# Layer 0's routing: the latents' lists sorted earlier, the last block of modulation products later, the first gather ahead of the late weight loads

## The chip, the cores and the metric

The kernel runs on one core of one Trainium2 chip. The metric is the device time of one execution in microseconds (us), lower is better. Every time below is that of one core.

## What is computed

A two-layer diffusion backbone over 512 latent tokens and 256 context tokens of width 1024. Each layer has a mixer (attention and a short convolution, ending in an output projection `w_out`) and an expert-choice mixture of experts (MoE). The part around the change is the seam between the two:

```python
x = x + g1 * ox                                   # ox: output projection
hx2 = _rmsnorm(x, norm2[l]) * (1.0 + sc2) + sh2
x = x + g2 * _ec_moe(hx2, router[l], ...)
...
def _ec_moe(h, router, w_gate, w_up, w_down):     # once for latents, once for context
    cap = CAPACITY_FACTOR * n // N_EXPERTS        # 64 of 512 latents, 32 of 256 context
    aff = softmax(h @ router)
    g, idx = top_k(swapaxes(aff, 1, 2), cap)      # per expert: its best tokens
    xs = h[idx]
    y = (silu(xs @ w_gate) * (xs @ w_up)) @ w_down * g
```

All scales and shifts (`sc2`, `sh2`, `g1` and so on) come from a modulation `silu(c) @ w_ada[l] + b_ada[l]`. Of the next layer's modulation the first 2048 columns are computed during this seam of layer 0.

## The kernel before

Every engine has its own instruction list, written out by hand; between them only semaphores set the order. The seam works on tiles of 128 tokens: layer 0 has six (t = 0 to 3 latents, t = 4 and 5 context), layer 1 has four (latents only). `NX` is 4, the number of latent tiles.

For each tile TensorE multiplies by `w_out` (`mixed_rows`, L1360, in pieces of k = 0 to 3, 4 to 5, 6 to 7). Behind the first piece of tile t stand the transposes of the normed tile t-1 (`turned_rows`, L1376), behind the second its router logits (`logit_parts`, L1388), behind the third their turn (`logits`, L1397). VectorE (DVE) scales and adds the residual (L1970, L1971, semaphore `x1`), takes a reciprocal (L1977) of the root that ScalarE (ACT) made of the squared sum (L1038, L1039), and writes half of the modulated transposed tile `o_h` (L1988); ACT writes the normed row (L1042, semaphore `oxn`) and the other half of `o_h` (L1050).

Between these DVE does two other works in layer 0:

- `ahead_sums(u)`, u = 0 to 7 (L1676): four products of 128x1024 with a summed output, next layer's modulation. Two units per latent tile, one after the reciprocal, one after `o_h`. Their weights come in 1 MB loads, two slots, issued by GpSimd (POOL) in `load_ahead` (L765).
- the latents' lists: `shifted`, `affinities` (softmax over experts, with ACT's Exp at L1045), the turn on TensorE (`turn_lists`, L1404), then eight rounds of `best_eight` (L1918 to L1921), each finding the next eight tokens of every half list. Rounds 0 to 3 stand in tile 4, rounds 4 to 7 in tile 5. Then `slots_out` (L1929, L1930), TensorE's `slots_across` (L1412, L1413), and `latents_merged` (L1942 to L1949), whose `iT` holds the token numbers.

POOL then copies the numbers of expert 0 (L817) and gathers its 64 latent rows of 4 KB from DRAM (L828); it has stored every tile's residual and normed rows (L793, L797) and waits for all of these stores first. TensorE turns the gathered rows (L1534), DVE modulates them (`first_latents`, L2075, L2076), and the MoE's first products start (`part_of`, L1510). The context's lists are sorted in four rounds around that.

SyncE (SP) loads all expert weights in units of 1 MB into a ring of 12 slots and some places of the arena that are free later. In layer 0 the units from the 13th on (`EARLY` is 0: four of `w_down`, two of `w_up`) wait until `o_h` and all the stores are done (L687 to L692), then they are issued.

Of the kernel before, what the change touches and what calls it, by code (L numbers as in the profile page):

```python
# [20 lines left out]
ALU = mybir.AluOpType  # L21
# [50 lines left out]
def build_program(nc, x, ctx, w_ada, w_adat, w_ahead, c_rows, w_in, w_out, router, w_gate, w_up, w_down, norm_final, small_in, rope, numbers, out):  # L72
# [102 lines left out]
    ahead_p = area(BIG + 16640, D).bitcast(BF16).rearrange("p (a k) -> p a k", a=2)  # L175
# [99 lines left out]
    s_ahead_c = sem("ahead_c_rows")  # L275
    s_ahead_mod = sem("ahead_mod_complete")
# [203 lines left out]
    LISTS_AT, MERGED_AT = 3840, 256  # L480
# [148 lines left out]
    def _(sp):  # L629
# [13 lines left out]
        for l in range(DEPTH):  # L643
# [33 lines left out]
            def load_long(which, expert, m0):  # L677
                for q in range(4):
                    m = m0 + q
                    dst, sem_of, _ = long_place(l, m)  # L680
                    if m < RING:
                        sp.wait_ge(free, spent(base) + m + 1 - RING)
                    elif m >= TURN[l]:
                        sp.wait_ge(free, spent(base) + m + 1 - TURN[l])
                    if m == RING + EARLY[l]:
                        sp.wait_ge(free, spent(where[("wout", l)]) + 4)
                        if l < DEPTH - 1:  # L687
                            sp.wait_ge(*LS[l]("ot", nq(l)))
# [21 lines left out]
    def _(pool):  # L710
# [28 lines left out]
        for l in range(DEPTH):  # L739
# [50 lines left out]
            for t in range(nq(l)):  # L790
                if l < DEPTH - 1:
                    pool.wait_ge(*L("x1", t + 1))
                    pool.dma_start(res[toks(t), :], o_x[t % 3]).then_inc(L[f"stx{t % 3}"], 16)  # L793
                    if 1 <= t < NX:
                        load_ahead(2 * t + 1)
                pool.wait_ge(*L("oxn", t + 1))
                pool.dma_start(xnd[toks(t), :], row_n(l, t)).then_inc(L[f"stn{t % 2}"], 16)  # L797
                if l < DEPTH - 1 and t < NX - 1:
                    load_ahead(2 * t + 2)
                if l < DEPTH - 1 and t + 3 < nq(l):  # L800
                    pool.wait_ge(*L(f"stx{t % 3}", 16 * (t // 3 + 1)))
                    pool.dma_start(o_x[t % 3], rows(t + 3)).then_inc(L[f"ox{t % 3}"], 16)
            for j in range(3 if l < DEPTH - 1 else 0):
                pool.wait_ge(*L(f"stx{j}", 16 * len(range(j, nq(l), 3))))
            for j in range(2):
                pool.wait_ge(*L(f"stn{j}", 16 * len(range(j, nq(l), 2))))
# [20 lines left out]
            if l < DEPTH - 1:  # L827
                pool.indirect_dma_start(out=xg[l][0:CAPX, :], out_offset=None, in_=xnd,  # L828
                                        in_offset=bass.IndirectOffsetOnAxis(ap=gidx[0:CAPX, 0:1], axis=0)
                                        ).then_inc(L["gl"], 16)  # L830
                pool.wait_ge(*L("ri", 2))
# [77 lines left out]
    def _(act):  # L909
# [11 lines left out]
        for l in range(DEPTH):  # L921
# [108 lines left out]

            act.wait_ge(s_norm[1], l + 1)
            for t in range(nq(l)):
                s = stream(t)
                act.wait_ge(*L("x1", t + 1))
# [8 lines left out]
                if t == NX:  # L1043
                    act.wait_ge(*L("asub", 1))
                    act.activation(aff[:, 0:NX, :], aff[:, 0:NX, :], ACT.Exp).then_inc(L["aexp"], 1)  # L1045
# [21 lines left out]
            n_col = 512 if l == DEPTH - 1 else 768  # L1067

# [19 lines left out]
    def _(pe):  # L1088
# [37 lines left out]
        for l in range(DEPTH):  # L1126
# [280 lines left out]
            def slots_across(g):  # L1407

                pe.wait_ge(*L("pad", g + 1))
                for r0 in list_groups(l)[g][2]:  # L1410
                    b, off = (5, 0) if r0 == 64 else (7 - r0 // 32, MERGED_AT)
# [4 lines left out]
            for i in range(nq(l) + 1):  # L1416
                if i < nq(l):
                    if i >= 2:
                        pe.wait_ge(*L("x1", i - 1))
                    mixed_rows(i, range(0, 4))  # L1420
# [4 lines left out]
                if i == NX + 1:  # L1425
                    turn_lists(0)
# [12 lines left out]
            else:  # L1439
                slots_across(0)  # L1440
# [158 lines left out]
    def _(dve):  # L1599
# [68 lines left out]
        def ahead_sums(u):  # L1668
# [3 lines left out]
            for o in range(4 * u, 4 * u + 4):  # L1672
# [3 lines left out]
                stt(ahead_p[:, o % 2, :], ahead_w[u % AHEAD_SLOTS][:, c % 2, :], 1.0, ahead_c[:, s, :], ALU.mult, ALU.mult,  # L1676
# [36 lines left out]
        for l in range(DEPTH):  # L1713
# [223 lines left out]
            low_v, low_i = [bank(7, NE, MERGED_AT + n * NE) for n in (0, 1)]  # L1937
            ctx_v, ctx_i = [bank(5, NE, n * NE) for n in (0, 1)]

            def latents_merged():  # L1940
                dve.wait_ge(*L("rows", 1))
                dlink(dve, dve.tensor_copy(high[:], bank(6, 2 * NE, MERGED_AT)))  # L1942
# [19 lines left out]
            for t in range(nq(l)):  # L1962
# [3 lines left out]
                if last and t >= 2:  # L1966
                    dve.wait_ge(*L("ot", t - 1))
                    dve.wait_ge(*L(f"stn{t % 2}", 16 * (t // 2)))
                part = row_n(l, t) if last else o_t
                dlink(dve, tt(part, bank(2 * (t % 2), D), g1row[s], ALU.mult))  # L1970
                tt(row_x(l, t), row_x(l, t), part, ALU.add).then_inc(L["x1"], 1)  # L1971
                if t == NX:
                    shifted(0)
                if t == NX + 1:
                    best_eight(0, 4)
                dve.wait_ge(*L("ort", t + 1))
                dve.reciprocal(stat[:, 2, t:t + 1], stat[:, 1, t:t + 1]).then_inc(L["orc"], 1)  # L1977
                if not last and t < NX:
                    ahead_sums(2 * t)
                if t == NX:  # L1980
                    affinities(0)
                if t == NX + 1:
                    best_eight(0, 5)
                dve.wait_ge(*L("ot", t + 1))
# [6 lines left out]
                if not last and t < NX:  # L1991
                    ahead_sums(2 * t + 1)
                if t == NX:
                    lists_in(0)
                    for r in range(4):
                        best_eight(0, r)
                if t == NX + 1:
                    best_eight(0, 6)
                    best_eight(0, 7)
# [7 lines left out]
            slots_out(0)  # L2007
# [80 lines left out]
            else:  # L2088
# [10 lines left out]
                first_context()  # L2099
            for e, par in body_experts(dve):  # L2100
# [96 lines left out]
```

## Time and profile before

| what | value |
|---|---|
| time before, median of 3 runs (lowest to highest) | 1933.68 us (1932.34 to 1934.58) |
| the profiled execution's own time | 1933.66 us |
| its span (first to last instruction) | 1931.5 us |
| TensorE busy | 1775.9 us, 92% of the span |
| DVE, ACT, POOL busy | 787.8, 369.1, 232.4 us |
| mean granted TensorE clock | 0.969 |
| layer 0's seam (first to last of its TensorE work) | about 399 to 527 us |
| layer 1's seam | about 1350 to 1445 us |

TensorE is busy for nearly the whole span, so what a change can win lies in the stretches in which it stands still. In a row of the timeline the bracket at the end tells how long the engine stood idle before it and what released it.

### The profile page before, as it was taken

To read this page: it belongs to the slowest core of one execution; us is meant where nothing else is said; L and a number is where in the kernel's file an instruction comes from. 1 tells how busy PE (TensorE), PEld (TensorE's weight loads), DVE (VectorE), ACT (ScalarE), POOL (GpSimd) and SP (SyncE) were. 2 spreads that over 40 slices of the span, in tenths; PEclk is the share of its full clock that TensorE was granted. 3 is DMA by queue.
4 is the path that set the end of the run, shared out by engine and by line. 5 is a ranking of instruction groups with operands and counts; after the bars stand their busy time and mean duration, and the time that the engine had idled before them with its cause. 6 is when DMAs were issued, how large, how long until landed. Compare 5 with 4: busy or idle time off the path is not lost.

```text
span 1931.5 us, 31131 instructions
## 1 busy us (share of the span) xinstructions
PE 1775.9 (92%) x13332; PEld 922.2 (48%) x13332; DVE 787.8 (41%) x1631; ACT 369.1 (19%) x801; POOL 232.4 (12%) x316
## 2 busy tenths in 40 slices
PE   6999999989599999999999999999949999889896
PEld 3886567744344444444443876577423332222221
DVE  2995665648611111111111664765242332323233
ACT  3213455622300000000001313555220000000001
POOL 1000330011011111212121001420000000000000
PEclk8999998999799999999999999999969999999998
DMA  9543000075779999999997843000579999999995
GB/s 386 217 153 153 1 1 1 2 319 204 267 276 393 396 393 396 392 395 393 393 393 312 317 167 131 1 23 25 218 286 388 404 404 413 404 410 404 411 412 232
DMA packets 83074, 525.69 MB, mean 272 GB/s; under 512 B 11280, under 2 KB 13600, under 8 KB 24064
## 3 DMA queue, kind: packets, MB, share of 16 engines
q1 hardware_dynamic: 65952, 476.17, 61.4%
q0 software_dynamic: 14784, 47.33, 7.9%
q8 instruction: 105, 1.72, 0.4%
q10 hardware_dynamic: 2208, 0.26, 0.1%
q14 instruction: 25, 0.20, 0.0%
HBM read 506.94 MB, written 16.79 MB: 271 GB/s over the span
## 4 chain that ended last, share of the span: by engine, by line
PE 75%; DMA 16%; DVE 4%; ACT 3%; issue 1%; SPq 0%; POOL 0%; DVEq 0%; ACTq 0%; POOLq 0%
PE psum L1471 16%; PE psum L1465 9%; PE psum L1474 8%; DMA ring<-in_w_up 7%; PE psum L1187 6%; PE psum L1360 6%; DMA arena<-in_w_up 6%; PE psum L1151 6%; PE psum L1263 5%; PE psum L1310 3%; PE psum L1281 3%; PE psum L1237 2%; PE psum L1553 2%; ACT arena L1004 2%; PE psum L1221 1%
## 5 line engine op out<-in xcount | busy, mean ns | idle before, releaser
L1471 PE MATMUL psum<-ring,arena 128*32 128x512 f32 x1920 | 250.4, 593 | 0.0
L1465 PE MATMUL psum<-ring,arena 128*64 128x512 f32 x976 | 228.5, 603 | 23.2 <-DMA ring<-in_w_down 12.9
L1072 ACT ACTIVATE arena<-psum 128x768 f32<-128x768 f32 (+1 forms) x32 | 22.5, 704 | 941.6 <-PE psum L1474 463.5
L1474 PE MATMUL psum<-ring,arena 128*32 128x256 f32 x1920 | 147.6, 379 | 0.0
L1465 PE MATMUL psum<-arena 128*64 128x512 f32 x560 | 132.2, 606 | 15.8 <-DMA arena<-in_w_down 6.6
L1360 PE MATMUL psum<-ring,arena 128*128 128x512 f32 x320 | 144.5, 603 | 0.0
L1465 PEld LDWEIGHTS psum<-ring,arena 128*64 128x64 f32 x976 | 63.8, 137 | 168.9 <-issue 117.7
L1004 ACT ACTIVATE arena<-psum,smx 128x768 f32<-128x768 f32 (+4 forms) x160 | 118.9, 748 | 107.6 <-DVE smx L1791 107.3
L1791 DVE TENSOR_REDUCE smx<-psum 128x1 f32<-128x768 f32 (+4 forms) x160 | 115.8, 765 | 39.0 <-PE psum L1221 27.9
L1474 PEld LDWEIGHTS psum<-ring,arena 128*32 128x32 f32 x1920 | 62.4, 110 | 143.6 <-issue 143.6
L1471 PE MATMUL psum<-arena 128*32 128x512 f32 x960 | 125.2, 593 | 0.0
L772 POOL TENSOR_SCALAR arena<-arena,smx 128x768 f32<-128x768 f32 (+1 forms) x40 | 77.9, 1947 | 368.9 <-DVE smx L1852 368.9
L1187 PE MATMUL psum<-ring,arena 128*128 128x256 f32 x544 | 120.8, 383 | 0.0
L1263 PE MATMUL psum<-arena,ring 128*128 128x512 f32 (+1 forms) x288 | 116.2, 545 | 1.6 <-ACT arena L1013 1.5
L1659 DVE SCALAR_TENSOR_TENSOR arena<-ring 128x1024 bf16<-128x1024 f32 x96 | 111.5, 1218 | 7.8 <-DMA ring<-in_w_adat 7.7
L1151 PE MATMUL psum<-ring,arena 128*128 128x256 f32 x512 | 114.0, 383 | 0.0
L2069 DVE TENSOR_TENSOR arena<-arena,psum 128x512 f32<-128x512 f32 x120 | 74.4, 681 | 89.1 <-PE psum L1553 89.1
L1187 PEld LDWEIGHTS psum<-ring,arena 128*128 128x128 f32 x544 | 103.8, 192 | 14.0
L1151 PEld LDWEIGHTS psum<-ring,arena 128*128 128x128 f32 x512 | 97.5, 192 | 13.0
L2060 DVE SCALAR_TENSOR_TENSOR arena<-psum,gcur,arena 128x512 f32<-128x512 f32 x15 | 11.3, 751 | 219.0 <-PE psum L1474 219.0
L1360 PEld LDWEIGHTS psum<-ring,arena 128*128 128x128 f32 x320 | 59.7, 193 | 68.0 <-issue 68.0
L2034 DVE TENSOR_TENSOR arena<-psum,arena 128x768 f32<-128x768 f32 (+1 forms) x32 | 26.4, 824 | 157.7 <-PE psum L1474 123.6
(286 smaller groups left out, 2067.3 us busy)
## 6 DMA issues: line engine op xcount, KB each, us to landing
ring<-in_w_gate SPq DMA_DIRECT2D x88, 1024.0 KB, 28.1
ring<-in_w_up SPq DMA_DIRECT2D x84, 1024.0 KB, 28.1
ring<-in_w_down SPq DMA_DIRECT2D x82, 1024.0 KB, 28.5
arena<-in_w_down SPq DMA_DIRECT2D x46, 1024.0 KB, 28.4
arena<-in_w_up SPq DMA_DIRECT2D x44, 1024.0 KB, 28.2
arena<-in_w_gate SPq DMA_DIRECT2D x40, 1024.0 KB, 28.5
ring<-in_w_adat SPq DMA_DIRECT2D x32, 1024.0 KB, 5.6
ring<-in_w_in SPq DMA_DIRECT2D x18, 1024.0 KB, 18.3
```

Source lines behind the costliest of these rows:

```text
L772: pool.tensor_scalar(p0, p0, smx[:, 2, u % 8:u % 8 + 1], None, ALU.mult).then_inc(L["first"], 1)
L1004: act.activation(p, scored(st, x), ACT.Exp, bias=smx[:, 0, u % 8:u % 8 + 1], accum_out=smx[:, 1, u % 8:u % 8 + 1]).then_inc(L["exp"], 1)
L1151: ins = mm(dst, hT[:, k, toks(t)], slot(where[("winA", l)] + j, 8)[:, k, :], start=k == 0, stop=k == KD - 1)
L1187: ins = mm(dst, hT[:, k, toks(t)], slot(where[("winD", l)] + j, 8)[:, k, :], start=k == 0, stop=k == KD - 1)
L1263: ins = mm(bank(6, n), slot(where[("winC", l, tile)], 8)[:, k, cc * P:(cc + 1) * P], hT[:, k, t0:t0 + n], start=k == 0, stop=k == KD - 1)
L1360: ins = mm(bank(2 * (t % 2) + n), mixc(k)[:, toks(t)], slot(wo + k // 2, 2)[:, k % 2, n * 512:(n + 1) * 512], start=k == 0, stop=k == KD - 1)
L1465: ins = mm(psum[64 * n:64 * n + 64, b * 512:(b + 1) * 512], lhs(k), w[:, n * 512:(n + 1) * 512], start=k == 0, stop=k == KD - 1)
L1471: ins = mm(psum[r0:r0 + 32, b * 512:(b + 1) * 512], lhs(k)[:, 32 * g:32 * g + 32], w[:, n * 512:(n + 1) * 512], start=k == 0, stop=k == KD ...
L1474: ins = mm(psum[32 * j:32 * j + 32, (b + 1) * 512:(b + 1) * 512 + 256], lhs_c(k), w[:, j * 256:(j + 1) * 256], start=k == 0, stop=k == KD - 1)
L1659: stt(products[:, o % 3, :], long_slot(l, u % LONG_SLOTS)[:, j, :], 1.0, c_row(l, s), ALU.mult, ALU.mult, accum_out=mod[:, l, LONG_CHUNK + ...
L1791: dve.tensor_reduce(smx[:, 0, u % 8:u % 8 + 1], scored(st, x), axis=AX_X if st.kind == "W" else AX_XY, op=ALU.max, negate=True).then_inc(L ...
L2069: ins = tt(half, half, bank(sums_at(part, blk, h)), ALU.add)
```

## The change

1. DVE, layer 0: of `ahead_sums` tile 0 has one unit instead of two, behind `o_h`. Every later unit stands one place later, and the last unit (7) stands behind the MoE's `first_context`. `load_ahead` moves accordingly on POOL, and the last unit's scratch `ahead_p` gets another place. ACT's first Silu waits for all sums.
2. DVE, tiles 4 and 5: `shifted` stands ahead of tile 4's residual, `affinities` ahead of its reciprocal, round 0 ahead of its `o_h`, rounds 1 to 4 behind it; rounds 5, 6, 7 and `slots_out` stand ahead of tile 5's `o_h`. TensorE turns the lists inside tile 5's first piece and does `slots_across` ahead of tile 5's logits. The merged lists lie in PSUM banks 3 and 2 instead of 7 and 6.
3. ACT: Sqrt's table is loaded once at the start of the seam; Exp for the latents stands ahead of tile 4, with Sqrt's table loaded again behind it; Exp's table is loaded right after the last tile's normed row.
4. POOL waits, before the first gather, for the stores of the four latent tiles only; it signals `s_first_gather` behind the gather, and SP's late loads wait for that too.

```diff
 # SP
                         sp.wait_ge(free, spent(where[("wout", l)]) + 4)
                         if l < DEPTH - 1:
+                            sp.wait_ge(s_first_gather, 1)
                             sp.wait_ge(*LS[l]("ot", nq(l)))
...
 # POOL
                     if 1 <= t < NX:
-                        load_ahead(2 * t + 1)
+                        load_ahead(2 * t)
                 pool.wait_ge(*L("oxn", t + 1))
                 pool.dma_start(xnd[toks(t), :], row_n(l, t)).then_inc(L[f"stn{t % 2}"], 16)
-                if l < DEPTH - 1 and t < NX - 1:
-                    load_ahead(2 * t + 2)
+                if l < DEPTH - 1 and 1 <= t < NX:
+                    load_ahead(2 * t + 1)
...
             for j in range(2):
-                pool.wait_ge(*L(f"stn{j}", 16 * len(range(j, nq(l), 2))))
+                pool.wait_ge(*L(f"stn{j}", 16 * len(range(j, NX, 2))))
...
                                         ).then_inc(L["gl"], 16)
+                pool.sem_inc(s_first_gather, 1)
+                for j in range(2):
+                    pool.wait_ge(*L(f"stn{j}", 16 * len(range(j, nq(l), 2))))
...
 # ACT
+            act.activation(rootx[:], eps[:], ACT.Sqrt)
             act.wait_ge(s_norm[1], l + 1)
             for t in range(nq(l)):
                 s = stream(t)
+                if t == NX:
+                    act.wait_ge(*L("asub", 1))
+                    act.activation(aff[:, 0:NX, :], aff[:, 0:NX, :], ACT.Exp).then_inc(L["aexp"], 1)
+                    act.activation(rootx[:], eps[:], ACT.Sqrt)
                 act.wait_ge(*L("x1", t + 1))
...
-                if t == NX:
-                    act.wait_ge(*L("asub", 1))
-                    act.activation(aff[:, 0:NX, :], aff[:, 0:NX, :], ACT.Exp).then_inc(L["aexp"], 1)
+                if t == nq(l) - 1:
+                    act.activation(rootx[:], eps[:], ACT.Exp)
...
+            if l < DEPTH - 1:
+                act.wait_ge(ahead_sum, 4 * AHEAD_UNITS)
...
 # TensorE
-                    mixed_rows(i, range(0, 4))
+                    if i == NX + 1:
+                        mixed_rows(i, range(0, 3))
+                        turn_lists(0)
+                        mixed_rows(i, range(3, 4))
+                    else:
+                        mixed_rows(i, range(0, 4))
...
-                if i == NX + 1:
-                    turn_lists(0)
+                if i == NX + 2:
+                    slots_across(0)
...
 # DVE
+                if t == NX:
+                    shifted(0)
                 part = row_n(l, t) if last else o_t
                 dlink(dve, tt(part, bank(2 * (t % 2), D), g1row[s], ALU.mult))
                 tt(row_x(l, t), row_x(l, t), part, ALU.add).then_inc(L["x1"], 1)
                 if t == NX:
-                    shifted(0)
-                if t == NX + 1:
-                    best_eight(0, 4)
-                dve.wait_ge(*L("ort", t + 1))
-                dve.reciprocal(stat[:, 2, t:t + 1], stat[:, 1, t:t + 1]).then_inc(L["orc"], 1)
-                if not last and t < NX:
-                    ahead_sums(2 * t)
-                if t == NX:
                     affinities(0)
                 if t == NX + 1:
                     best_eight(0, 5)
+                dve.wait_ge(*L("ort", t + 1))
+                dve.reciprocal(stat[:, 2, t:t + 1], stat[:, 1, t:t + 1]).then_inc(L["orc"], 1)
+                if not last and 1 <= t < NX:
+                    ahead_sums(2 * t - 1)
+                if t == NX:
+                    lists_in(0)
+                    best_eight(0, 0)
+                if t == NX + 1:
+                    best_eight(0, 6)
+                    best_eight(0, 7)
+                    slots_out(0)
                 dve.wait_ge(*L("ot", t + 1))
...
                 if not last and t < NX:
-                    ahead_sums(2 * t + 1)
+                    ahead_sums(2 * t)
                 if t == NX:
-                    lists_in(0)
-                    for r in range(4):
+                    for r in range(1, 5):
                         best_eight(0, r)
-                if t == NX + 1:
-                    best_eight(0, 6)
-                    best_eight(0, 7)
...
                 first_context()
+                ahead_sums(AHEAD_UNITS - 1)
```

DVE's list in layer 0, tile 0 and the start of tile 1, before. L1970 and L1971 are the residual, L1977 the reciprocal, L1676 the `ahead_sums` products, L1988 `o_h`:

```order
L1970 TENSOR_TENSOR arena<-psum,arena 128x1024 [waits ox0,po,gxe]
L1971 TENSOR_TENSOR arena<-arena 128x1024 [waits dve_chain]
L1977 RECIPROCAL stat<-stat 128x1 [waits ort]
L1676 SCALAR_TENSOR_TENSOR arena,mod<-arena 128x1024 [waits ahead_landed0,ahead_c_rows]
L1676 SCALAR_TENSOR_TENSOR arena,mod<-arena 128x1024
L1676 SCALAR_TENSOR_TENSOR arena,mod<-arena 128x1024 [waits ahead_sum] x2
L1988 TENSOR_SCALAR arena<-psum,acol,mod 128x128 [waits ot]
L1988 TENSOR_SCALAR arena<-psum,acol,mod 128x128 x3
L1676 SCALAR_TENSOR_TENSOR arena,mod<-arena 128x1024 [waits ahead_sum,ahead_landed1]
L1676 SCALAR_TENSOR_TENSOR arena,mod<-arena 128x1024 [waits ahead_sum] x3
L1970 TENSOR_TENSOR arena<-psum,arena 128x1024 [waits ox1,po]
```

And the same stretch in the changed kernel, where L1988, L1989, L1995, L2009 and L1692 are these lines:

```order
L1988 TENSOR_TENSOR arena<-psum,arena 128x1024 [waits ox0,po,gxe]
L1989 TENSOR_TENSOR arena<-arena 128x1024 [waits dve_chain]
L1995 RECIPROCAL stat<-stat 128x1 [waits ort]
L2009 TENSOR_SCALAR arena<-psum,acol,mod 128x128 [waits ot]
L2009 TENSOR_SCALAR arena<-psum,acol,mod 128x128 x3
L1692 SCALAR_TENSOR_TENSOR arena,mod<-arena 128x1024 [waits ahead_landed0,ahead_c_rows]
L1692 SCALAR_TENSOR_TENSOR arena,mod<-arena 128x1024
L1692 SCALAR_TENSOR_TENSOR arena,mod<-arena 128x1024 [waits ahead_sum] x2
L1988 TENSOR_TENSOR arena<-psum,arena 128x1024 [waits ox1,po]
```

Tile 0's `o_h` no longer stands behind a product that waits for a load, and the tile has four products instead of eight.

DVE's list at the end of the seam, from tile 5's residual add on, before (L1918, L1919, L1921 are one round, L1929 and L1930 `slots_out`):

```order
L1971 TENSOR_TENSOR arena<-arena 128x1024 [waits dve_chain]
L1918 MAX vals<-arena 48x8
L1919 MAX_INDEX idx<-vals,arena 48x8 [waits dve_chain]
L1921 MATCH_REPLACE arena<-vals,arena 48x256 [waits dve_chain]
L1977 RECIPROCAL stat<-stat 128x1 [waits ort,dve_chain]
L1918 MAX vals<-arena 48x8
...
L1988 TENSOR_SCALAR arena<-psum,acol,mod 128x128 [waits lg,ot,dve_chain]
L1988 TENSOR_SCALAR arena<-psum,acol,mod 128x128 x3
L1918 MAX vals<-arena 48x8
...
L1918 MAX vals<-arena 48x8 [waits dve_chain]
L1919 MAX_INDEX idx<-vals,arena 48x8 [waits dve_chain]
L1929 COPY vpad<-vals 16x128 [waits dve_chain]
```

And in the changed kernel (L1989 the residual add, L1934 to L1937 one round, L1945 and L1946 `slots_out`, L2009 `o_h`):

```order
L1989 TENSOR_TENSOR arena<-arena 128x1024 [waits dve_chain]
L1934 MAX vals<-arena 48x8
...
L1995 RECIPROCAL stat<-stat 128x1 [waits ort,dve_chain]
L1934 MAX vals<-arena 48x8
...
L1934 MAX vals<-arena 48x8 [waits dve_chain]
L1935 MAX_INDEX idx<-vals,arena 48x8 [waits dve_chain]
L1945 COPY vpad<-vals 16x128 [waits dve_chain]
L1946 TENSOR_SCALAR vpad<-vals 16x128
L1945 CAST ipad<-idx 16x128
L1946 TENSOR_SCALAR ipad<-idx 16x128
L2009 TENSOR_SCALAR arena<-psum,acol,mod 128x128 [waits lg,ot]
```

Behind the residual add there were four rounds, two of them behind `o_h`; now there are three, and `slots_out` stands ahead of `o_h`.

## Rows read from the trace of the kernel before

**Rows 1.** TensorE's waits, 395 to 560 us: total, times, longest.

```profile
PE psum L1534 <- DMA arena<-normed_rows,gidx: 7.6, 1, 7.6
PE psum L1388 <- DVE arena L1988: 6.3, 2, 4.8
```

**Rows 2.** Timeline, tiles 0 to 4: start, us, what, idle before.

```profile
397.70 1.07 POOL L765 DMA_DIRECT2D arena<-in_w_ahead  x2
...
420.98 3.60 PE L1360 MATMUL psum<-ring,arena 128*128 128x512 f32 x8
...
423.28 1.23 DVE L1676 SCALAR_TENSOR_TENSOR arena<-arena 128x1024 bf16<-128x1024 f32 x1 [4.47 <-DMA arena<-in_w_ahead]
...
427.86 1.37 DVE L1988 TENSOR_SCALAR arena<-psum,acol,mod 128x128 f32<-128x128 f32 x4
...
429.38 1.08 PE L1388 MATMUL psum<-arena,rout 128*32 128x128 f32 x16 [4.80 <-DVE arena L1988]
...
436.06 7.11 PE L1360 MATMUL psum<-ring,arena 128*128 128x512 f32 x16
...
439.43 0.53 POOL L765 DMA_DIRECT2D arena<-in_w_ahead  x1
...
443.88 3.60 PE L1360 MATMUL psum<-ring,arena 128*128 128x512 f32 x8
...
446.41 1.23 DVE L1676 SCALAR_TENSOR_TENSOR arena<-arena 128x1024 bf16<-128x1024 f32 x1 [0.23 <-DMA arena<-in_w_ahead]
...
451.67 7.11 PE L1360 MATMUL psum<-ring,arena 128*128 128x512 f32 x16
...
482.87 7.11 PE L1360 MATMUL psum<-ring,arena 128*128 128x512 f32 x16
```

**Rows 3.** Windows: us, busy by engine, granted clock, DMA share, GB/s.

```profile
425.00:430.00 5.00, 0.62 (x13) 0.66 (x16) 5.00 (x11) 0.00 (x0) 0.53 (x1) 0.76 1.00 397
```

**Rows 4.** DMA issues, 395 to 440 us: count, KB each, median us to landing.

```profile
arena<-in_w_ahead POOLq DMA_DIRECT2D x4, 1024.0 KB, 16.6
```

**Rows 5.** Timeline, tile 5 and the routing behind it.

```profile
498.86 1.23 DVE L1970 TENSOR_TENSOR arena<-psum,arena 128x1024 f32<-128x1024 f32 x1 [0.31 <-DVE arena L1921]
...
502.55 1.28 ACT L1039 ACT_TABLE_LOAD   x1
...
505.64 1.55 PE L1376 MATMUL psum<-ident,arena 128*128 128x128 f32 x8 [4.64 <-ACT arena L1042]
...
508.57 0.41 DVE L1918 MAX8 vals<-arena 48x8 f32<-48x256 f32 x1
...
511.02 0.21 DVE L1929 COPY vpad<-vals 16x128 f32<-16x128 f32 x1
...
513.09 0.19 DVE L1942 COPY high<-psum 128x32 f32<-128x32 f32 x1 [1.16 <-PE psum L1413]
...
514.01 0.17 DVE L1947 CAST iT<-token 64x16 uint32<-64x16 f32 x1
...
514.38 0.17 DVE L1885 TENSOR_REDUCE affm<-psum 128x2 f32<-128x32 f32 x1
...
515.11 0.97 POOL L828 DMA_INDIRECT arena<-normed_rows,gidx  x1 [0.58 <-POOL gidx L817]
...
519.42 0.40 DVE L1921 MATCH_REPLACE8 arena<-vals,arena 16x256 f32<-16x256 f32 x1
...
524.00 1.09 PE L1534 MATMUL psum<-ident,arena 64*128 64x64 f32 x8 [7.61 <-DMA arena<-normed_rows,gidx]
...
526.71 6.97 PE L1510 MATMUL psum<-ring,arena 128*32 128x512 f32 x48 [1.62 <-issue]
```

**Rows 6.** Timeline of SP in layer 0's seam.

```profile
509.12 2.00 SPq L693 DMA_DIRECT2D arena<-in_w_down  x4
```

**Rows 7.** Timeline, layer 1: its first gather of 64 rows.

```profile
1438.92 0.98 POOL L823 DMA_INDIRECT arena<-normed_rows,gidx  x1 [0.28 <-POOL gidx L817]
...
1442.83 1.11 PE L1450 MATMUL psum<-ident,arena 64*128 64x64 f32 x8 [3.78 <-DMA arena<-normed_rows,gidx]
```

**Rows 8.** Timeline, start of layer 0's MoE.

```profile
548.07 1.02 DVE L2020 TENSOR_TENSOR arena<-psum,acol 128x512 f32<-128x512 f32 x2 [5.25 <-PE psum L1450]
...
551.44 1.04 PE L1471 MATMUL psum<-ring,arena 128*32 128x512 f32 x8
```

More of the change, by code:

```diff
@@ L174, in build_program @@
     ahead_c = area(BIG + 14336, 2, D)
-    ahead_p = area(BIG + 16640, D).bitcast(BF16).rearrange("p (a k) -> p a k", a=2)
+    ahead_p = [area(at, D).bitcast(BF16).rearrange("p (a k) -> p a k", a=2) for at in (BIG + 16640, BIG + 7424)]
     sqd = area(BIG + 8448, 2, T)
@@ L275, in build_program @@
     s_ahead_c = sem("ahead_c_rows")
+    s_first_gather = sem("first_gather_issued")
     s_ahead_mod = sem("ahead_mod_complete")
@@ L478, in list_groups @@
         return [latents, (NX, NB, (64,), CAPC)] if l < DEPTH - 1 else [latents]
-    LISTS_AT, MERGED_AT = 3840, 256
+    LISTS_AT = 3840
     def signals(l):
@@ L827, in _ @@
             if l < DEPTH - 1:
-                pool.indirect_dma_start(out=xg[l][0:CAPX, :], out_offset=None, in_=xnd,
+                pool.indirect_dma_start(out=xg[l][0:CAPX, :], out_offset=None, in_=xnd[0:SEQ, :],
                                         in_offset=bass.IndirectOffsetOnAxis(ap=gidx[0:CAPX, 0:1], axis=0)
                                         ).then_inc(L["gl"], 16)
+                pool.sem_inc(s_first_gather, 1)
+                for j in range(2):
+                    pool.wait_ge(*L(f"stn{j}", 16 * len(range(j, nq(l), 2))))
                 pool.wait_ge(*L("ri", 2))
@@ L1410, in slots_across @@
                 for r0 in list_groups(l)[g][2]:
-                    b, off = (5, 0) if r0 == 64 else (7 - r0 // 32, MERGED_AT)
+                    b, off = (5, 0) if r0 == 64 else (3 - r0 // 32, 0)
                     mm(bank(b, NE, off), vpad[r0:r0 + NE, :], sel[r0:r0 + NE, :], start=True, stop=True)
@@ L1439, in _ @@
             else:
-                slots_across(0)
                 turn_lists(1)
@@ L1675, in ahead_sums @@
                     dve.wait_ge(ahead_sum, o - 1)
-                stt(ahead_p[:, o % 2, :], ahead_w[u % AHEAD_SLOTS][:, c % 2, :], 1.0, ahead_c[:, s, :], ALU.mult, ALU.mult,
+                stt(ahead_p[u == AHEAD_UNITS - 1][:, o % 2, :], ahead_w[u % AHEAD_SLOTS][:, c % 2, :], 1.0, ahead_c[:, s, :], ALU.mult, ALU.mult,
                     accum_out=mod[:, 1, c, s:s + 1]).then_inc(ahead_sum, 1)
@@ L1935, in slots_out @@
                 ins.then_inc(L["pad"], 1)
-            low_v, low_i = [bank(7, NE, MERGED_AT + n * NE) for n in (0, 1)]
+            low_v, low_i = [bank(3, NE, n * NE) for n in (0, 1)]
             ctx_v, ctx_i = [bank(5, NE, n * NE) for n in (0, 1)]
@@ L1941, in latents_merged @@
                 dve.wait_ge(*L("rows", 1))
-                dlink(dve, dve.tensor_copy(high[:], bank(6, 2 * NE, MERGED_AT)))
+                dlink(dve, dve.tensor_copy(high[:], bank(2, 2 * NE)))
                 tt(first[:], low_v, high[:, 0:NE], ALU.is_ge)
@@ L2006, in _ @@
                     best_eight(0, r)
-            slots_out(0)
+                slots_out(0)
             latents_merged()
```

## The prediction

> **What bounds the kernel now.** TensorE is busy for 92% of the span, so I asked where it stands still. Its list of waits over layer 0's seam names two places that matter: 7.6 us for the first gather, and 6.3 us for DVE's `o_h`, 4.8 of them at once [rows 1]. I then followed each in the timeline.
>
> The first place is tile 0. TensorE ends the second piece of tile 1 at 420.98 + 3.60 = 424.58 and stands until 429.38, because DVE writes tile 0's `o_h` only at 427.86: ahead of it stand four `ahead_sums` products, which began at 423.28, when their weights landed [rows 2]. There the granted clock is 0.76 on average, so it is at the lower of its two levels (1.2 GHz) for part of that stretch [rows 3], and the rest of tile 1 is slow.
>
> The second place is the end of the seam. From tile 5's residual at 498.86 a single chain runs: residual, ACT's root with a table load of 1.28, normed row, transposes at 505.64, `o_h`, two rounds of the sort, `slots_out` at 511.02, merge, `iT` at 514.01, gather issued at 515.11. The gathered rows are used only at 524.00, and the MoE starts at 526.71 [rows 5]. SP issued its late loads of 1 MB from 509.12 on, ahead of the gather [rows 6]. Layer 1's gather of the same 64 rows took 1442.83 - 1438.92 = 3.91 from its issue to TensorE's first use, against 524.00 - 515.11 = 8.89 in layer 0 [rows 7, 5].
>
> What lies behind the seam frees ring slots only as TensorE goes on, and SP loads only into freed slots, so I take it that all of it moves as a whole when the MoE starts earlier.
>
> **Part 1: tile 0's order.** Without a stall it takes 451.67 - 443.88 = 7.79 from the start of a second piece to the next tile. In tile 1 it took 436.06 - 420.98 = 15.08 [rows 2]. With `o_h` right behind the transposes DVE would write it from about 421.1 on, for 1.37, before TensorE asks at 424.58. The gain is 15.08 - 7.79 = **7.3 us**: the wait of 4.8, and 2.5 of work at the lower clock.
>
> What is late next? The four products of unit 0 last 427.86 - 423.28, about 4.6 [rows 2], to 427.9. Tile 2 would start at 420.98 + 7.79 = 428.8, so 0.9 of cover is left. In tiles 1 to 3 DVE still has two units each, and every load takes another's old place in both lists: the unit used behind `o_h` is now issued right behind the residual's store, where the one issued at 439.43 was used at 446.41 after a wait of 0.23 [rows 2]. The first of them may come 1 us late, since POOL is held by tile 0's store until the burst of loads has drained; I put DVE's spare time at 0.5 and TensorE's at 1.2 per tile and cost it at nothing, bounded by 1.
>
> Unit 7 moves behind `first_context`: 4.6, and about 0.4 for bias and scales, 5.0 in all. DVE is idle there for 5.25 before expert 1's rows, and TensorE wants these at 551.44, 1.3 after DVE has them (548.07 and two steps of 1.02) [rows 8]. Cost nothing, bounded by 0 and 1. ACT's first Silu waits for these sums too; it is wanted at 551.44 as well.
>
> **Part 2: tile 4**, in the old time base. TensorE starts tile 5's first piece at 482.87 and ends it 7.11 later, at 490.0 [rows 2]. DVE puts `shifted` (0.5) ahead of the residual. From a residual's start to the transposes it takes 505.64 - 498.86 - 1.28 = 5.50 without a table load [rows 5], so the normed row is there at 482.9 + 0.5 + 5.5 = 488.9, 1.1 before it is wanted. The softmax (0.8 behind the residual's 2.5) ends at 486.7; the turn wants it three quarters into the piece, at 488.2. ACT's two switches (1.28 each) and Exp end at 485.6, as the residual does at 485.9. DVE then has the lists at 489.0, round 0 until 490.5, `o_h` until 492.5 and four rounds of about 1.5, until 498.4; the residual waits for TensorE until 498.86 as before. Nothing is lost, with margins of 0.3 to 1.5.
>
> **Part 3: from 498.86 on.** The table load is gone, so the transposes start at 505.64 - 1.28 = 504.4. DVE has rounds 6 and 7 from 503.1 on (511.02 - 508.57 = 2.45 for a long and a short one), `slots_out` from 505.6, and the merge could start 513.09 - 511.02 = 2.07 later, at 507.7; `o_h` lies in between and ends at 507.9. The merge takes 514.18 - 513.09 = 1.09: `iT` at 509.0 instead of 514.2. With the same 0.93 for POOL's copy the gather is issued at **509.9** instead of 515.11 [rows 5], 5.2 earlier. Tile 5's residual store is still waited for; I take it to have landed by then, since SP waited for it too and issued at 509.12 [rows 6].
>
> Then the gather itself. The late loads are held until it is issued, so I take layer 1's 3.91: rows at 513.8 instead of 524.00. Now DVE is later than they are: the context's list starts with the last logits at about 510.1 and takes 519.82 - 514.38 = 5.44 to the end of its second round [rows 5], to 515.5, and `first_latents` stands behind it. From the transposes' end to the first product it was 526.71 - 525.09 = 1.6, so the MoE starts at 517.1 instead of 526.71: **9.6 us**.
>
> The late loads are issued 1.8 later than before, at 510.9. Six of them, 6.3 MB at the 397 GB/s of [rows 3], take 16, to 527. `w_down` of expert 0 is used behind 551.44 in the old order [rows 8], behind 541.8 in the new. The cover is some 15 us.
>
> **Part 4: tables in layer 1.** Exp's load there lay almost beside DVE's work and tile 0's Sqrt load beside matmuls. I give 0.2, bounds 0 and 1.3 (one load).
>
> A rule weighed. In the row the load takes 1.28, and the 5.50 above takes off no more [rows 5]. The Trainium skill ("ScalarE: Activation LUTs", What ACT_TABLE_LOAD costs) adds a drain of about 1380 ns to the load's 1283, 2.66 us per switch. By that, taking one away in tile 5 would give 1.4 more, and the two in tile 4 would take 5.3 and end behind the residual, which would eat the margin there; the trace of before has no such gap around its load.
>
> **The sum.** 7.3 + 9.6 + 0.2 = 17.1, against the profiled execution's own 1933.66 (the runs' median is 1933.68, so nothing to correct): 1916.6.
>
> **The rivals.**
>
> *The gather isn't protected.* SP issues as soon as the gather's instruction is through. If its loads crowd the rows as now, the gather keeps its 8.89: 509.9 + 8.9 = 518.8, and 2.7 to the first product, 521.5. The gain there is 5.2, in all 12.7: **1921.0**. For it: the loads and the gather share the DMA engines. Against it: the loads start behind the rows, not ahead. Chance 0.17.
>
> The Trainium skill ("DMA: Bandwidth & Descriptors", Queues, rings and completion order) says that a DMA engine goes round robin between its queues, packet by packet. By this a burst ahead or behind would cost 64 rows little, and holding back the loads would win little by itself, as in this rival; the 8.89 against 3.91 speaks against it.
>
> *Tile 0's stall only moves*, to tile 1's `o_h`. Only 9.8 is left: **1923.9**. Against it: 0.9 us to spare above. Chance 0.07; both this and the one before, 1928.3, chance 0.02.
>
> *The gap is short enough to keep the clock.* TensorE stands for 3.4 instead of 4.64 before the transposes; work at the upper level would give 1 to 2.5 more, about **1915**. Chance 0.10.
>
> *Slower: late modulation loads.* In the burst the first load, issued at 397.70, was used at 423.28 [rows 2], and the median to landing was 16.6 [rows 4], against 7.0 in the quiet case. If the loads behind the residual's store took 16.6 in tiles 1 to 3, each tile would lose 9.6 less 1.2: 25 in all, 1916.6 + 25 = **1942**. It decides from 17.1 / 3 + 1.2 + 7.0 = 14 us per load on. Against it: the burst has drained by tile 1's end, and later tiles load the same amount as before. Chance 0.03 for slower, 0.02 for a partial case within 0.2%.
>
> **The numbers.** The forecast has 0.59, the rivals what is given. A measurement of this kernel can tell about 0.2%, 3.9 us, from no change. Faster 0.95, same 0.02, slower 0.03. The range reaches from the kept clock to the unprotected gather, with 1 us beyond each: 1914 to 1922. Outside lie the 1923.9 case, the double one and the slow ones.
>
> **What the profile after would show.** No wait of TensorE for `o_h` in tile 0, and its clock whole between 425 and 435; tile starts 15.6 apart and 7.3 earlier from tile 2 on; no table load between tile 5's residual and its normed row; the gather issued 5.2 + 7.3 = 12.5 before 515.11, at 502.6, its rows used 4 us later or when DVE is through the context's second round; the first product at about 509.8; SP's late loads right behind the gather; no new wait for expert 1's rows. I am wrong if the gather still takes 8 us, if a modulation load makes `o_h` late in tiles 1 to 3, or if TensorE waits for `afft` in tile 5.

## The result

The changed kernel takes 1925.83 us (median of 8 runs, 1922.01 to 1930.63) beside 1936.68 for the kernel before on the same chip (8 runs): ratio 0.9946, 95% interval 0.9933 to 0.9959. It is faster by 0.54%, about 10.5 us (the medians lie 10.85 apart), where 17.1 were forecast, and lies outside the range. Its profiled execution took 1923.94 us, span 1922.1.

The difference lies in layer 0's seam. I measure it from the gate transposes (TensorE turns the mixer's gate `g1` into rows, the seam's first step; 395.61 us before, 396.79 after) to the MoE's first product (526.71 and 517.41): 131.10 before, 120.62 after, 10.5 less. Behind it the two spans run 1404.8 and 1404.7; ahead of it the changed kernel was 1.2 us later in its profiled execution, in work that the change doesn't touch. The gate transposes, before and after:

```profile
395.61 3.84 PE L1333 MATMUL psum<-ident,mod 128*128 128x128 f32 x32 [0.38 <-DVE arena L1807]
...
396.79 3.84 PE L1345 MATMUL psum<-ident,mod 128*128 128x128 f32 x32 [0.38 <-DVE arena L1823]
```

TensorE's waits in the stretch of [rows 1], of the kernel after:

```profile
PE psum L1550 <- DMA arena<-normed_rows,gidx: 6.4, 1, 6.4
PE psum L1388 <- ACT arena L1052: 5.6, 2, 3.4
PE psum L1526 <- issue: 1.6, 1, 1.6
PE psum L1416 <- DVE afft L1910: 1.5, 1, 1.5
PE psum L1400 <- DVE arena L2009: 0.5, 2, 0.4
```

The 6.3 for `o_h` are down to 0.5, as meant. The gather's wait is still 6.4, where 7.6 stood before, and `L1388 <- ACT` comes twice, where one (3.4) was expected. Two things went otherwise than forecast, then.

The window of [rows 3], after. TensorE is busy throughout, at the upper level:

```profile
425.00:430.00 5.00, 5.00 (x29) 2.42 (x28) 4.01 (x9) 0.28 (x1) 0.00 (x0) 1.00 1.02 404
```

The timeline of tiles 0 to 3 after, POOL, DVE and TensorE (compare [rows 2]):

```profile
420.19 0.53 POOL L799 DMA_DIRECT2D normed_rows<-arena  x1 [2.40 <-ACT arena L1052]
433.38 0.53 POOL L804 DMA_DIRECT2D arena<-in_x  x1 [12.66 <-DMA residual<-arena]
433.90 0.53 POOL L795 DMA_DIRECT2D residual<-arena  x1
434.42 0.53 POOL L767 DMA_DIRECT2D arena<-in_w_ahead  x1
...
422.15 1.37 DVE L2009 TENSOR_SCALAR arena<-psum,acol,mod 128x128 f32<-128x128 f32 x4 [3.44 <-PE psum L1388]
424.12 1.23 DVE L1692 SCALAR_TENSOR_TENSOR arena<-arena 128x1024 bf16<-128x1024 f32 x1 [0.61 <-DMA arena<-in_w_ahead]
...
444.63 1.23 DVE L1692 SCALAR_TENSOR_TENSOR arena<-arena 128x1024 bf16<-128x1024 f32 x1 [4.78 <-DMA arena<-in_w_ahead]
...
429.72 7.11 PE L1372 MATMUL psum<-ring,arena 128*128 128x512 f32 x16
...
445.33 7.11 PE L1372 MATMUL psum<-ring,arena 128*128 128x512 f32 x16
454.64 1.09 PE L1388 MATMUL psum<-ident,arena 128*128 128x128 f32 x8 [2.20 <-ACT arena L1052]
455.57 3.60 PE L1372 MATMUL psum<-ring,arena 128*128 128x512 f32 x8
...
463.58 7.11 PE L1372 MATMUL psum<-ring,arena 128*128 128x512 f32 x16
```

`o_h` is written at 422.15, ahead of the products, and tile 2 starts at 429.72 instead of 436.06. But the products of unit 2 wait 4.78 at 444.63 for a load that POOL issued at 434.42. POOL stood from 420.72 to 433.38 for the landing of tile 0's residual store, and the load now has its place behind that wait and behind tile 1's residual store. Tile 2's normed row comes late by this, TensorE waits 2.20 for it at 454.64, and tile 4 starts at 463.58, 18.25 behind tile 3 instead of 15.60.

The end of the seam after (compare [rows 5] and [rows 6]):

```profile
499.42 1.15 ACT L1052 ACTIVATE arena<-arena,stat 128x1024 f32<-128x1024 f32 x1 [0.30 <-DVE stat L1995]
500.58 1.28 ACT L1054 ACT_TABLE_LOAD   x1
501.88 0.20 ACT L1054 ACTIVATE rootx<-eps 128x1 f32<-128x1 f32 x1
...
500.62 1.97 PE L1388 MATMUL psum<-ident,arena 128*128 128x128 f32 x8 [3.35 <-ACT arena L1052]
...
504.89 0.17 DVE L1963 CAST iT<-token 64x16 uint32<-64x16 f32 x1
...
505.84 1.97 SPq L695 DMA_DIRECT2D arena<-in_w_down  x4
...
505.99 0.97 POOL L830 DMA_INDIRECT arena<-normed_rows,gidx  x1 [0.58 <-POOL gidx L819]
...
514.70 1.08 PE L1550 MATMUL psum<-ident,arena 64*128 64x64 f32 x8 [6.38 <-DMA arena<-normed_rows,gidx]
515.89 0.69 DVE L2092 TENSOR_TENSOR arena<-psum,acol 128x512 f32<-128x512 f32 x1 [4.14 <-PE psum L1550]
...
517.41 7.07 PE L1526 MATMUL psum<-ring,arena 128*32 128x512 f32 x48 [1.62 <-issue]
```

The gather is issued 109.20 behind the gate transposes; before it was 119.50. But SP's first late load begins at 505.84, 0.15 ahead of the gather's own row, and the gather takes 514.70 - 505.99 = 8.71, where 8.89 stood before.

The steps between follow. The second gates are TensorE's next such transposes, behind tile 5 (498.83 before, 495.09 after).

| step, us | before | after | gain | forecast |
|---|---|---|---|---|
| gate transposes to tile 2 | 40.45 | 32.93 | 7.52 | 7.3 |
| tile 2 | 15.61 | 15.61 | 0 | 0 |
| tile 3 | 15.60 | 18.25 | -2.65 | 0, at most -1 |
| tile 4 to the second gates | 31.56 | 31.51 | 0.05 | 0 |
| second gates to tile 5's transposes | 6.81 | 5.53 | 1.28 | 1.3 |
| from there to the gather's issue | 9.47 | 5.37 | 4.10 | 3.9 |
| issue to first use | 8.89 | 8.71 | 0.18 | 5.0 |
| first use to the first product | 2.71 | 2.71 | 0 | -0.6 |

### The profile page after: what moved, and what is told of

It reads as the page before. It is cut to its first block, busy times and chain, and to the rows that moved or that the text cites. A ratio compares the mean times of both kernels' runs of the same rounds, so it can differ in the third digit from the quotient of the medians.

```text
span 1922.1 us, 31140 instructions
## 1 busy us (share of the span) xinstructions
PE 1776.2 (92%) x13332; PEld 923.5 (48%) x13332; DVE 788.4 (41%) x1631; ACT 370.2 (19%) x806; POOL 232.5 (12%) x316
## 4 chain that ended last, share of the span: by engine, by line
PE 74%; DMA 17%; DVE 5%; ACT 3%; issue 1%; SPq 0%; POOL 0%; DVEq 0%; POOLq 0%; ACTq 0%
PE psum L1487 16%; PE psum L1481 9%; PE psum L1490 8%; DMA ring<-in_w_up 7%; PE psum L1199 6%; DMA arena<-in_w_up 6%; PE psum L1163 6%; PE psum L1372 5%; PE psum L1275 5%; PE psum L1322 3%; PE psum L1293 3%; PE psum L1249 2%; PE psum L1569 2%; ACT arena L1009 2%; PE psum L1233 1%
## 5 line engine op out<-in xcount | busy, mean ns | idle before, releaser
L1163 PEld LDWEIGHTS psum<-ring,arena 128*128 128x128 f32 x512 | 98.5, 194 | 13.2
```

The costliest lines, as they stand in the source:

```text
L1163: ins = mm(dst, hT[:, k, toks(t)], slot(where[("winA", l)] + j, 8)[:, k, :], start=k == 0, stop=k == KD - 1)
```

## The experiments

Theory A: the late loads get ahead of the gather, since the signal that frees them comes too early. Its rival B: layer 0's gather is slow by itself. Theory C: POOL, held by the residual store, issues unit 2's load too late. Its rival D: the DMA engines can't bring that load earlier. The ratios are to the kernel before, run on the same chip; seams and their parts come from one profiled execution of each kernel.

### The hold moved to the landing, and taken away

```diff
--- e1_loads_after_rows, against the changed kernel
-                            sp.wait_ge(s_first_gather, 1)
+                            sp.wait_ge(*LS[l]("gl", 16))
...
-                pool.sem_inc(s_first_gather, 1)
```

> The changed kernel, but SP's late loads wait until the first gather's rows have landed, not only for the signal behind its issue. Theory A (the 8.7 us of the gather come from the late loads, which start before its rows are through): the gather takes about 3.9 us from issue to first use as in layer 1, DVE's second context round (ends 5.4 us behind the last logits) then holds first_latents, and the MoE starts some 4.2 us earlier than in the changed kernel: about 1921.6 against its 1925.8 in the timed runs; no later wait appears, since expert 0's w_down has some 10 us of cover left. Theory B (layer 0's gather is slow by itself, for example because its rows were only just stored): it keeps 8 to 9 us, and the time stays within 1 us of the changed kernel's.

Measured: 1923.59, ratio 0.9943 (0.9929 to 0.9956). TensorE in tile 3, then the gather with POOL, SP and TensorE:

```profile
454.33 1.92 PE L1387 MATMUL psum<-ident,arena 128*128 128x128 f32 x8 [2.28 <-ACT arena L1051]
456.04 4.50 PE L1371 MATMUL psum<-ring,arena 128*128 128x512 f32 x8
...
507.13 0.97 POOL L830 DMA_INDIRECT arena<-normed_rows,gidx  x1 [0.58 <-POOL gidx L819]
...
511.41 1.92 SPq L695 DMA_DIRECT2D arena<-in_w_down  x4
...
511.48 1.09 PE L1549 MATMUL psum<-ident,arena 64*128 64x64 f32 x8 [2.02 <-DMA arena<-normed_rows,gidx]
```

The gather takes 4.35 instead of 8.71: A, not B. From its issue to the first product it is now 7.32, 4.1 less. Tile 3, though, took 19.78 here, 1.5 more than in the changed kernel, so the seam is only 2.6 shorter (118.05), and the ratio shows no difference; about 4.2 us were expected. The 1.5 come from TensorE's clock: it waits 2.28 here and 2.20 in the changed kernel, but the granted clock in 450 to 460 us is 0.83 here and 1.00 there, and the same work that takes 1.09 and 3.60 us there takes 1.92 and 4.50 here.

e2_no_hold takes away both the wait and the signal.

> The changed kernel without SP's wait for the gather's signal: the late loads go as soon as tile 5's stores have landed, some 2 us before the gather's issue. Theory A: they are further ahead of the gather's rows; 8.7 to 9.5 us from issue to use. If the signal did protect the gather by some amount, that amount is lost here. Theory B: the gather's 8.7 unchanged. In both the seam's end moves by less than 1 us, since the signal came at 505.84, before the gather's own span began at 505.99, and so held the loads back by only some 2 us.

One run, 1928.88. The loads begin 2.16 ahead of the gather, which takes 9.21. The hold as it was written moved the loads by 2.0 us and is worth 0.5 us at most: the four kernels with it took 8.55 to 9.03 (the table at the end), which is as wide a scatter. The seam is 124.56, because tile 3 took 21.69 here.

### The signal behind an operation that POOL's pipe must finish

```diff
--- e3_signal_behind_alu, against the changed kernel
-                pool.sem_inc(s_first_gather, 1)
+                pool.tensor_tensor(perch[:, 3, :], perch[:, 4, :], perch[:, 4, :], ALU.add).then_inc(s_first_gather, 1)
```

> The changed kernel, but the signal hangs on a small GpSimd operation behind the gather, which starts when the gather's span of about 1 us is over. Theory A in the form that the signal only came too early: SP's loads start some 1.2 us later, behind all of the gather's descriptors, and the gather needs 3.9 to 5 us. Theory A in the form that the loads crowd the rows even from behind: the gather still takes 6 to 8.7 us. Theory B: 8.7 unchanged.

One run, 1924.84. POOL, SP and TensorE at the gather:

```profile
508.58 0.99 POOL L830 DMA_INDIRECT arena<-normed_rows,gidx  x1 [0.58 <-POOL gidx L819]
509.58 0.18 POOL L833 TENSOR_TENSOR perch<-perch 1x2 f32<-1x2 f32 x1
...
509.84 2.27 SPq L695 DMA_DIRECT2D arena<-in_w_down  x4
...
513.05 1.09 PE L1550 MATMUL psum<-ident,arena 64*128 64x64 f32 x8 [2.13 <-DMA arena<-normed_rows,gidx]
```

The added operation runs only when the gather's row has ended, and SP starts 1.26 behind the start of that row instead of 0.15 ahead of it. That is enough: the gather takes 4.47, and 7.33 to the first product, the same as with the hold to the landing. The seam stays at 120.62, since unit 2's load made DVE wait 6.83 here and TensorE 4.24, with work at the lower clock behind it; tile 3 took 22.36, and the second fault took back what mending the first gave.

### The kernel before with the landing's hold alone

```diff
--- e7_before_held, against the kernel before
                         if l < DEPTH - 1:
+                            sp.wait_ge(*LS[l]("gl", 16))
```

> The kernel before, in its old order, with one line more: SP's late loads wait until the first gather's rows have landed. Theory A: the gather takes 3.9 to 4.4 us instead of 8.9, the context's two rounds are over by then (5.4 us from their start at the merge), so the seam from gate transposes to the first product shrinks from 131.1 by 4.5 to 5.2 us, to about 126.3, with nothing of the change in it; some 1931 in the timed runs where the kernel before has 1935.4. Theory B (the faster gather needs something else of the changed kernel): 131.

Measured: ratio 0.9982 (0.9969 to 0.9996). The gather takes 3.89, as in layer 1 [rows 7], and the seam 125.40, which is 5.7 less (1.0 of it ahead of tile 2). From the gather's issue to the first product it is 6.59 instead of 11.60: one line is worth 5.0, about half of what the whole change gave in the seam.

### Unit 2's load in time

```diff
--- e4_unit2_early, against the changed kernel
-                    if 1 <= t < NX:
+                    if 2 <= t < NX:
                         load_ahead(2 * t)
...
-                if l < DEPTH - 1 and 1 <= t < NX:
-                    load_ahead(2 * t + 1)
+                if l < DEPTH - 1 and t < NX:
+                    load_ahead(2 * t + 1 if t else 2)
```

> The changed kernel, but POOL issues the load of modulation unit 2 already in tile 0 (behind its normed row's store, when unit 0 is summed, ahead of the residual load for tile 3). Theory C (the 4.8 us that DVE waits for it come from POOL standing 12.7 us for the first residual store, so that the load goes out at 434.4 together with four others): the load goes out at about 429, DVE's wait and TensorE's 2.2 us in tile 2 vanish, tile 3 starts 2.6 us earlier, about 1923.2 in the timed runs. Theory D (the DMA engines cannot bring unit 2 any earlier, since the burst is still draining): DVE still waits 2 us or more and TensorE's start of tile 3 gains under 1 us.

Measured: 1921.72, ratio 0.9931 (0.9917 to 0.9945). POOL's timeline, and the starts of tiles 3 and 4 on TensorE:

```profile
428.18 0.54 POOL L767 DMA_DIRECT2D arena<-in_w_ahead  x1 [8.62 <-DVE arena L1692]
432.81 0.53 POOL L804 DMA_DIRECT2D arena<-in_x  x1 [4.09 <-DMA residual<-arena]
...
444.17 7.11 PE L1372 MATMUL psum<-ring,arena 128*128 128x512 f32 x16
459.77 7.11 PE L1372 MATMUL psum<-ring,arena 128*128 128x512 f32 x16
```

Issued at 428.18, as soon as unit 0 has freed the slot and ahead of the wait for the store, the load is there when DVE wants it; neither DVE nor TensorE waits, and the tiles stand 15.6 apart. The seam is 118.30. Not D; and C, in that the load must stand ahead of that wait. The gather, unprotected here, takes 9.03.

### Part 1 alone, as it is and mended

e5_products_only is the kernel before with the changed places of the loads and products. e10_products_unit2_early adds the edit of e4.

> The kernel before with the first part of the change alone: the modulation products and their loads one place later, unit 7 behind first_context. By the trace of the changed kernel: TensorE's wait in tile 0 and its slow clock are gone (7.5 us from the gate transposes to tile 2's start), and DVE's wait for unit 2's load takes 2.2 to 4.2 us of it back in tile 2. From the gate transposes to the MoE's first product 131.1 us in the kernel before; here 125.3 to 126.8. If the late load came from the rest of the change (its other store and table order) and not from this part, the full 7.5 stands: 123.6. The rest of the seam as before: a table load in tile 5's chain, the gather 8.9 us.

> The kernel before with part 1 alone (as e5_products_only) and unit 2's load issued in tile 0 behind the normed store. Theory C (GpSimd, held for the first residual store, issues unit 2's load too late, and this is what took part 1's 7.3 back): the 5.68 us wait of VectorE for that load goes, tile 3 to 4 takes 15.6 instead of 20.6, the seam is 124.0 instead of 129.05, and the ratio is 0.9964 (0.995 to 0.998). Theory D (the DMA engines could not bring it earlier, whenever it is issued): VectorE still waits 3 us or more there, the seam stays above 127, the ratio 0.998 to 1.000.

Measured: 0.9990 (0.9977 to 1.0003) without the edit, 0.9962 (0.9945 to 0.9979) with it. Without it, POOL's and DVE's timeline:

```profile
435.06 0.54 POOL L802 DMA_DIRECT2D arena<-in_x  x1 [12.04 <-DMA residual<-arena]
...
436.11 0.53 POOL L765 DMA_DIRECT2D arena<-in_w_ahead  x1
...
446.74 1.23 DVE L1679 SCALAR_TENSOR_TENSOR arena<-arena 128x1024 bf16<-128x1024 f32 x1 [5.68 <-DMA arena<-in_w_ahead]
```

Tile 2 begins 7.3 earlier in both. Without the edit tile 3 takes 20.60, and 5.0 are given back, more than in the changed kernel; the seam is 129.05, above the 125.3 to 126.8 expected. With it tile 3 takes 15.61 and the seam is 123.67, 7.4 less than before's. So the order of tile 0 is worth its 7.3 only when the load behind it is moved too.

### Parts 2 and 3 without part 1

e8_lists_only and e8b_lists_only put the ahead units' loads and products back into their old places. The two have the same instructions. In the first, unit 7's scratch lies over rows of the gate (`g1row`) that are still in use; the second has the old scratch.

> The changed kernel with the modulation products and their loads in the old places (two units from tile 0 on, none behind first_context): the lists, tables and the signal alone. TensorE stands 4.8 us in tile 0 again, with the slow clock. From there on the trace of the changed kernel applies: 1.3 us for the table load out of tile 5's chain, 4.1 for slots_out ahead of o_h and the merge ahead of the logits, nothing at the gather. 131.1 - 5.5 = 125.6 from the gate transposes to the first product. If unit 7's products in tile 3 delayed the lists in tile 4, more would be lost: 127 or over.

> The change without part 1: the products and loads of the ahead units in their old places (unit 7 in tile 3 with the scratch it had before), everything else as in the changed kernel. This is e8_lists_only with unit 7's scratch moved so that nothing is overlaid. If the parts add up: tile 2 starts 39.8 to 40.5 us behind the gate transposes, the gather takes 8.7 to 9.2, the seam is 125.1, that is 6.0 less than before's 131.1, and the ratio is about 0.9970 (0.9955 to 0.9985). If the parts interact (the old tile 0 stall loosens or tightens later loads): the seam is off 125.1 by more than 1.5.

Measured: one run of 1931.11 for the first; ratio 0.9968 (0.9956 to 0.9980) for the second, seams 125.07 and 125.33. The gather is issued at 114.07 instead of 119.50 and takes 8.55. The parts add up nearly: 5.8 us here and 7.4 in e10 make 13.2, and e4, which has both, gained 12.8 (0.32% and 0.38% against 0.69%).

### Both faults mended

e9_both_mended is the changed kernel with the edits of e3 and e4.

> The changed kernel with both faults mended: the signal behind a small GpSimd operation, so that the late loads come 1.3 us later, and unit 2's load issued in tile 0. Both gains add: 118.3 (unit 2 early alone) less 4.1 = 114.2 us from the gate transposes to the first product, against 131.1 before: 16.9 us, the size of the forecast. In the timed runs 1935.4 - 16.9 = 1918.5, a ratio of 0.9913. If the two are not independent (the drained DMA queue of the one being needed by the other), it stays at 116 or more.

Measured: 1918.28, ratio 0.9913 (0.9899 to 0.9928), the fastest of all. POOL, SP, TensorE and DVE at the gather:

```profile
503.99 0.99 POOL L830 DMA_INDIRECT arena<-normed_rows,gidx  x1 [0.58 <-POOL gidx L819]
504.99 0.18 POOL L833 TENSOR_TENSOR perch<-perch 1x2 f32<-1x2 f32 x1
...
505.25 2.49 SPq L695 DMA_DIRECT2D arena<-in_w_down  x4
...
508.42 1.09 PE L1550 MATMUL psum<-ident,arena 64*128 64x64 f32 x8 [2.10 <-DMA arena<-normed_rows,gidx]
511.32 5.35 PE L1526 MATMUL psum<-ring,arena 128*32 128x512 f32 x24 [1.81 <-issue]
...
509.36 0.40 DVE L1937 MATCH_REPLACE8 arena<-vals,arena 16x256 f32<-16x256 f32 x1
509.80 0.69 DVE L2092 TENSOR_TENSOR arena<-psum,acol 128x512 f32<-128x512 f32 x1
```

The seam takes 113.88, 17.2 less than before; the medians lie 16.2 apart. `first_latents` now stands behind the second round of the context's list without a wait of its own, as the prediction had it, and the first product comes 7.33 behind the gather's issue (7.2 forecast).

## Why the prediction was wrong

**What bounds the kernel** and **all of it moves as a whole** held: the gain is the seam's. Behind the seam the profiled executions scatter from 1404.7 to 1410.6 without a pattern, so less than that isn't to be read there in one execution.

**Part 1, 7.3 us**: measured 7.52, and 7.3 in e5 and e10. The clock is whole in 425 to 430, and unit 0's products end at 428.8, 0.9 ahead of tile 2's start, the cover that was counted on.

**"The first of them may come 1 us late ... I ... cost it at nothing, bounded by 1"**: this is the first step that failed, in size. The mechanism was named, POOL held by tile 0's store, but its price wasn't worked out from the rows. DVE wanted the load at 444.63 - 4.78 = 439.85, and it was issued at 434.42. With the 7.0 of the quiet stretch it would have been there at 441.4, 1.6 late, not far from the 1 I had. But it took 10.2, 3.2 more, and the two make the wait of 4.8. I had taken the duration from a quiet stretch, though the wait in front of it ends in a burst. TensorE loses 2.65 in the changed kernel, 4.2 in e1, 5.0 in e5, 6.1 in e2 and 6.8 in e3, whose order is the same there. In these four it waits 2.28, 3.09, 2.93 and 4.24, and the rest is mostly work at the lower clock (granted 0.83 in e1 and 0.66 in e3 over 450 to 460 us, 1.00 in the changed kernel, which waits 2.20); the bound of 1 had no term for that. What stretches the load is, most likely, that POOL lets everything go at once. The DMA view of 428 to 450 us of the changed kernel (22 us in 40 slices, then the issues):

```profile
GB/s 395 410 335 402 328 410 350 201 22 30 15 0 209 141 276 276 365 432 365 305 313 223 253 290 320 350 402 410 439 432 387 402 417 246 164 112 60 45 22 0
...
arena<-in_w_ahead POOLq DMA_DIRECT2D x2, 1024.0 KB, 9.8
arena<-in_x POOLq DMA_DIRECT2D x1, 512.0 KB, 4.8
residual<-arena POOLq DMA_DIRECT2D x1, 512.0 KB, 5.5
normed_rows<-arena POOLq DMA_DIRECT2D x1, 512.0 KB, 10.4
arena<-in_ctx POOLq DMA_DIRECT2D x1, 512.0 KB, 9.9
```

The engines all but stand still for some 2 us (slices 9 to 12) until POOL is free; then six transfers, 4 MB in all, are issued within 6.4 us. With the load ahead of all that, in e4, e9 and e10, the loss is gone. That the company is what stretches a load is argued, not tested by itself: in e4, where unit 2's load isn't among the six, unit 3's, issued at 437.70 in the middle of the others, lands 7.9 behind its issue, where the two loads of the changed kernel need 10.2 and 9.5. Why the same load takes 9.7 (e1) to 11.5 us (e3) between kernels alike in this stretch isn't settled.

**The slower rival** ("late modulation loads", from 14 us per load on) is this mechanism in three tiles. The load took about 10, under the 14 it needed, and only tile 3 was hit: later loads are issued without a held POOL. The rival that the stall moves to tile 1's `o_h` was wrong in place: the load late next was the one two units on. That its 1923.9 is the profiled execution's 1923.94 is chance.

**Part 2, nothing lost**: 31.51 against 31.56 us. Tile 4's residual waits 0.44 for the fifth round, which costs TensorE nothing.

**Part 3 up to the gather's issue, 5.2**: 5.4 (1.28 and 4.10). TensorE stands 3.35 instead of 4.64 [rows 5] and then works at the lower clock (0.61 in 500 to 502, 0.50 from 502 to 514), so the case that the clock is kept didn't come. The 1.28 of the load are all that went: the activation behind the load at 500.58 starts at 501.88, with 0.02 between. The row ahead of the load ends at 500.57, so there is no gap on that side either. The drain of about 1380 ns that the Trainium skill adds to the load ("ScalarE: Activation LUTs", What ACT_TABLE_LOAD costs) doesn't show in this trace.

**"The late loads are held until it is issued, so I take layer 1's 3.91"**: this is the step that failed and cost most. The first rival, with 0.17, had it that the gather isn't protected. Its reason against, "the loads start behind the rows, not ahead", is what the trace refutes: the signal passes the gather. Mended, the gather takes 4.4 (3.9 where the loads wait for the landing), so the 3.91 itself was a fair price.

Together: 1916.6 + 4.8 (gather 8.71 instead of 3.91) + 2.65 (tile 3) = 1924.05, and the profiled execution took 1923.94. That it fits to 0.1 is partly luck: parts 1 and 3 gave 0.4 more than forecast, the step to the first product cost 0.6 less, and against these stand 1.2 lost ahead of the seam. With both faults mended the seam's forecast is met, and part by part: 7.5 up to tile 2, 5.4 up to the gather's issue and 4.3 from there to the first product, against 7.3, 5.2 and 4.4.

**Unit 7 behind `first_context`, nothing**: right. Its products run 533.54 to 538.2, expert 1's rows follow at 538.90, and TensorE has no wait there. **Part 4, 0.2**: nothing that small can be read behind the seam.

## What to carry to other kernels

A signal that stands in program order behind a DMA's issue is no proof that the DMA is ahead in the engines; put it on an operation that waits for the issue to be through, or wait for the landing, and look in the trace at which row comes first. When work is taken from an in-order queue and put behind another wait, follow that wait to its end in the trace and price the load from there, with all that is let go at the same moment; a bound of "at most 1" needs rows of its own. And measure a change's parts alone: here one part gave back 5.0 of its own 7.3, and two small edits took the gain from 0.54% to 0.87%.

## What the runs showed of the hardware

The gather of 64 rows costs one of two prices, by when SP's burst of 1 MB loads begins relative to the start of its own row (us, from issue to TensorE's first use):

| kernel | burst begins | gather |
|---|---|---|
| e5, e10 | -6.69 | 8.76, 8.34 |
| before | -5.99 | 8.89 |
| e2 | -2.16 | 9.21 |
| after, e4, e8, e8b | -0.15 | 8.71, 9.03, 8.93, 8.55 |
| e3, e9 | +1.26 | 4.47, 4.43 |
| e7, e1 | +3.81, +4.28 | 3.89, 4.35 |

Between -0.15 and +1.26 it falls by half, and neither an earlier nor a later start matters much. A burst that begins while the gather is still under way, at +1.26, costs it little (4.45 against 3.89 and 4.35); one ahead of it by 0.15 costs as much as one ahead by 6. The gather isn't behind all of the burst's bytes either: in the changed kernel the last two of the six loads landed 16.8 us (median) behind their issue at 507.85 and later. Round robin between queues, as the Trainium skill has it ("DMA: Bandwidth & Descriptors", Queues, rings and completion order), fits that it isn't behind all, but doesn't give why a burst ahead costs some 4.5 us and a burst in the middle next to nothing. What exactly the rows stand behind stays open.

A semaphore increment of GpSimd, written behind an indirect DMA, let SP start 0.15 us ahead of that DMA's row of 0.97, in each of the four profiles that have it (after, e4, e8, e8b); without it (e2) SP started 2.16 ahead.
